# A hybrid decoder layer: SSM output products by pairs of groups, turns of the identity in routing, and a tail that starts two blocks sooner

## The reference

```
h    = rms_norm(x, ln1_g);  proj = h @ w_in
a    = differential attention (4 heads, two softmax maps each, head norm)
c    = GLU, causal depthwise conv (31 taps), LayerNorm, silu
s    = S5 SSM: 16 channel groups x 64 complex states, GELU, GLU
x    = x + concat(a, c, s) @ w_out
h2   = rms_norm(x, ln2_g)
x    = x + MoE(h2)     # top 1 of 4 groups, then top 2 of its 8 experts
out  = rms_norm(x, final_g)
# expert: act = silu(xb @ w_gate[e]) * (xb @ w_up[e]);  y = act @ w_down[e]
```

## Time and profile before

| | |
|---|---|
| runs | 1229.65, 1231.2, 1232.02 us; median 1231.2 |
| the profiled execution | 1231.33 us, span 1229.6 us |
| mean granted clock of TensorE | 0.966 of 2.4 GHz |
| TensorE busy | 1142.1 us, 93% of the span |
| VectorE, ScalarE, GpSimd busy | 466.2, 366.2, 287.9 us |
| SSM output products | 265.6 to 282.6 us |
| routing, last logits to first expert block | 557 to 583.9 us |
| expert blocks | 583.9 to 1199 us |
| tail | 1199 to 1229.6 us |

### The profile page before, as it was taken

One profiled execution on the slowest core, in us unless ns is written; L12 is line 12 of the kernel. 1 busy time (PEld: TensorE's weight loads), 2 busy tenths in 40 slices (PEclk: granted clock), 3 DMA queues, 4 the chain that ended last, 5 costly groups with the idle time before them and its releaser, 6 DMA issues.

```text
span 1229.6 us, 16168 instructions
## 1 busy us (share of the span) xinstructions
PE 1142.1 (93%) x5022; PEld 547.6 (45%) x5023; DVE 466.2 (38%) x1011; ACT 366.2 (30%) x736; POOL 287.9 (23%) x227
## 2 busy tenths in 40 slices
PE   6999999998899999994899999987999999999990
PEld 5897444454346666654233333322333333333330
DVE  3550039942446666446222323312232332322313
ACT  3221100025455556412223232222322223323223
POOL 0110299920000000101022122222212212122123
PEclk9999999999899999997799999989999999999995
DMA  8127111012411111177692999999799999999217
GB/s 254 26 39 140 35 35 35 0 69 74 171 35 59 63 50 37 52 296 298 231 375 31 359 374 375 410 414 413 284 364 378 396 404 378 404 361 409 99 21 276
DMA packets 86157, 261.95 MB, mean 213 GB/s; under 512 B 31927, under 2 KB 49086, under 8 KB 61518
## 3 DMA queue, kind: packets, MB, share of 16 engines
q1 hardware_dynamic: 68868, 243.43, 51.6%
q0 software_dynamic: 11520, 16.81, 6.2%
q10 hardware_dynamic: 5706, 0.92, 0.4%
HBM read 244.86 MB, written 26.74 MB: 221 GB/s over the span
## 4 chain that ended last, share of the span: by engine, by line
PE 88%; DMA 5%; ACT 2%; DVE 2%; issue 1%; POOL 0%; SPq 0%; DVEq 0%; ACTq 0%; POOLq 0%
PE psum L1349 28%; PE psum L1368 14%; PE psum L1058 13%; PE psum L1248 9%; PE psum L1055 4%; PE psum L1202 3%; DMA W<-in_w_gate 3%; PE psum L1335 3%; PE psum L1222 3%; PE psum L1053 2%; PE psum L1356 2%; PE psum L1213 2%; PE psum L1277 1%; DMA W<-in_x 1%; PE psum L1266 1%
## 5 line engine op out<-in xcount | busy, mean ns | idle before, releaser
L1349 PE MATMUL psum<-W,RD 128*64 (+1 forms) x800 | 371.9, 609 | 15.4 <-DVE RD L1869 14.5
L1350 PE MATMUL psum<-W,RD 128*64 128x512 f32 x800 | 371.9, 609 | 0.0
L1349 PEld LDWEIGHTS psum<-W,RD 128*64 128x64 f32 x800 | 107.4, 140 | 229.0 <-issue 223.1
L1368 PE MATMUL psum<-W,RD 128*64 (+1 forms) x400 | 184.0, 603 | 2.3 <-ACT RD L981 2.3
L709 POOL DMA_INDIRECT x_rows<-RD,tabi x49 | 79.7, 1627 | 452.2 <-ACT RD L988 442.5
L1369 PE MATMUL psum<-RD 128*64 128x512 f32 x400 | 184.0, 603 | 0.0
L1851 DVE TENSOR_TENSOR RD<-psum,RD 128x256 f32<-128x256 f32 x50 | 21.3, 425 | 420.6 <-ACT RD L977 420.6
L1058 PE MATMUL psum<-W 128*128 128x512 f32 x384 | 166.4, 593 | 0.6 <-ACT W L794 0.6
L1248 PE MATMUL psum<-W,RD 128*128 128x512 f32 x256 | 119.9, 602 | 1.6 <-ACT RD L870 1.1
L1058 PEld LDWEIGHTS psum<-W 128*128 128x128 f32 x384 | 72.5, 190 | 89.7 <-issue 88.7
L1350 PEld LDWEIGHTS psum<-W,RD 128*64 128x64 f32 x800 | 107.4, 140 | 0.0
(11 more groups left out here) (324 smaller groups left out, 1269.3 us busy)
## 6 DMA issues: line engine op xcount, KB each, us to landing
W<-in_w_up SPq DMA_DIRECT2D x32, 2048.0 KB, 13.3
W<-in_w_gate SPq DMA_DIRECT2D x32, 2048.0 KB, 18.2
W<-in_w_down SPq DMA_DIRECT2D x32, 2048.0 KB, 20.1
W<-in_x SPq DMA_DIRECT2D x16, 512.0 KB, 4.7
W<-in_w_in SPq DMA_DIRECT2D x5, 1024.0 KB, 11.6
W<-in_w_in SPq DMA_DIRECT2D x16, 256.0 KB, 4.3
x_rows<-W SPq DMA_DIRECT2D x8, 512.0 KB, 2.9
h_rows<-RD SPq DMA_DIRECT2D x8, 512.0 KB, 3.6
```

What stands on the lines that cost most here:

```text
L1349: pe.matmul(bank(2)[0:HALF].rearrange("p (g n) -> p g n", g=2), x, near, start=k == 0, stop=k == KD - 1)
L1350: ins = pe.matmul(bank(2)[HALF:P], x, upgate1[:, k].rearrange("p g n -> p (g n)"), start=k == 0, stop=k == KD - 1)
L1368: pe.matmul(out[0:HALF], a, W[:, bass.ds(base + (2 * KD * FF + D * k), 512)], start=k == 0, stop=k == FK - 1)
```

## The change

Three parts.

1. The SSM output products go by pairs: for pair `a` first both groups' `XR` products, then both `XI` products, then both `TG` products. The sums and their places in PSUM are the same.
2. `spin(count)` issues so many turns of the identity into a PSUM bank that nobody reads: 36 behind the rank counts, 24 behind the four column turns. Two semaphores (`col_ok`, `col_ps`) are folded into `tab_ok` and `tab_ps`.
3. `block_io(b)` scatters block b-2 instead of b-1, ahead of the gather, so that the last two blocks are never scattered. SyncE loads the tiles of the tail when the scatters up to the third last block have landed (`sent` and `got` hold their counts). VectorE squares tiles 0 to 3 and ScalarE tiles 4 to 7. All eight tiles are scaled and stored, also rows that are not final. Apart from that GpSimd fetches the 128 half rows of the second last block (`rows_in(0)`), VectorE adds that block's output, GpSimd writes them back to `x2_rows`, fetches the rows of the last block (`rows_in(1)`), VectorE adds the last block's output straight from PSUM with its gate. Both row tiles are squared, the two halves of each token's mean are added across partitions, rooted and scaled with a half-wise copy of the gain (`fgh`), and written over the stored rows of `out` once all bulk stores have landed: `rows_out(0)`, then `rows_out(1)`.

```diff
+            out_half = t["out"][0].rearrange("n (h d) -> (n h) d", h=2)
             def block_io(b):
+                if b >= 2:
+                    pool.wait_ge(ex_ye, b - 1)
+                    if b >= 3:
+                        pool.wait_ge(scat_out[(b - 1) % 2], 16 * ((b - 1) // 2))
+                    add_rows(tabi[:, b - 2:b - 1], yb[b % 2], scat_out[b % 2])
                 pool.wait_ge(ex_xT, b + 1)
                 gather(b + AHEAD)
-                if b:
-                    pool.wait_ge(ex_ye, b)
-                    if b >= 2:
-                        pool.wait_ge(scat_out[b % 2], 16 * (b // 2))
-                    add_rows(tabi[:, b - 1:b], yb[(b - 1) % 2], scat_out[(b - 1) % 2])
...
-            sp.wait_ge(moe_done, 3 + AHEAD)
+            sp.wait_ge(scat_out[0], sent[0])
+            sp.wait_ge(scat_out[1], sent[1])
             for i in range(NT):
-                sp.dma_start(x3[:, i, :], x2_dram[i * P:(i + 1) * P, :]).then_inc(x3_in[i], 16)
+                sp.dma_start(x3[:, i, :], x2_dram[i * P:(i + 1) * P, :]).then_inc(x_in[i], 16)
...
+            pool.wait_ge(cur_c, 2)
+            for s in range(2):
+                pool.wait_ge(scat_out[s], got[AHEAD + s])
+            rows_in(0)
+            for i in range(4):
+                tile_root(i)
+            pool.wait_ge(yrow_ok[0], 1)
+            for i in range(NT):
+                pool.wait_ge(x_in[i], 32)
+            pool.indirect_dma_start(x2_half, bass.IndirectOffsetOnAxis(ap=cur[:, 0:1], axis=0), yrow[0], None,
+                                    bounds_check=2 * L - 1, oob_is_err=False).then_inc(scat_m, 16)
+            tile_root(4)
+            tile_root(5)
+            tile_root(6)
+            tile_root(7)
+            pool.wait_ge(scat_m, 16)
+            rows_in(1)
+            row_root(0)
+            pool.wait_ge(orow_ok, 1)
+            pool.wait_ge(fin_out, 16 * NT)
+            rows_out(0)
+            row_root(1)
+            pool.wait_ge(orow_ok, 2)
+            pool.wait_ge(row_out[0], 16)
+            rows_out(1)
...
-            y_evac(ylast, bank(6), act.snap(more + (EXPERTS - 1)), act.snap(more + EXPERTS), 0, None, tail_y)
-            for i in range(NT):
...
+            for i in range(4, NT):
+                act.wait_ge(x_in[i], 32)
...
+                act.activation(banks(2, 2), x3[:, i, :], ACT.Square, accum_out=ms3[:, i:i + 1]).then_inc(ms3_ok, 1)
...
+            for r in range(2):
+                act.wait_ge(yrow_ok[r], 1)
...
+                act.activation(bank(3), yrow[r], ACT.Square, accum_out=msx[:, r:r + 1]).then_inc(sqx_ok, 1)
...
-            for g in range(GROUPS):
...
+            for a in range(PAIRS):
+                out = [psum[:, 2 * r + a // 4, P * (a % 4):P * (a % 4) + P] for r in range(2)]
+                for X, CA, first in ((XR, CAR, True), (XI, CAI, False)):
+                    for r in range(2):
+                        q = slice(STATES * r, STATES * r + STATES)
+                        pe.matmul(out[r], X[q, a, :], CA[q, a, 1:CHUNK + 1, :].rearrange("p t h -> p (t h)"),
+                                  start=first, stop=False)
+                for r in range(2):
+                    ins = pe.matmul(out[r], UT[:, 2 * a + r, :], TG[:, 2 * a + r, :], start=False, stop=True)
+                if a % 4 == 3:
                     ins.then_inc(y_ps, 1)
...
+            def spin(count):
+                for _ in range(count):
+                    pe.transpose(bank(6)[:, 0:P], ident[:, :], ident[:, :])
...
             ins.then_inc(rank_ps, 1)
+            pe.wait_ge(head_ss, NI)
+            spin(36)
...
-            ins.then_inc(col_ps, 1)
+            ins.then_inc(tab_ps, 1)
+            spin(24)
...
+            for i in range(4):
+                dve.wait_ge(x_in[i], 32)
+                dve.tensor_tensor_reduce(out=sqjunk, in0=x3[:, i, :], in1=x3[:, i, :], scale=1.0, scalar=0.0,
+                                         op0=ALU.mult, op1=ALU.add, accum_out=ms3[:, i:i + 1]).then_inc(ms3d_ok, 1)
+                dve.wait_ge(ms3d_ok, i + 1)
+                tile_mean(i)
+            dve.wait_ge(xrow_in[0], 16)
+            dve.wait_ge(ex_ye, dve.snap(more + (EXPERTS - 1)))
+            dve.tensor_tensor(yrow[0], RD[:, bass.ds(odd_at + 3072, 512)], xrow[0], ALU.add).then_inc(yrow_ok[0], 1)
+            for i in range(NT):
+                if i >= 2 and i + 2 < NT:
+                    dve.wait_ge(ms3_ok, i - 1)
+                    tile_mean(i + 2)
+                tile_scale(i)
+            row_mean(0)
+            dve.wait_ge(xrow_in[1], 16)
+            dve.wait_ge(ex_y, dve.snap(more + EXPERTS))
+            dve.wait_ge(glast_ok, 1)
+            dve.scalar_tensor_tensor(yrow[1], bank(6), glast[:, :], xrow[1], ALU.mult, ALU.add).then_inc(yrow_ok[1], 1)
+            row_scale(0)
+            row_mean(1)
+            row_scale(1)
```

More of the change, by code:

```diff
@@ L223, in build @@
         x3 = W[:, 2 * SLOT:2 * SLOT + NT * D].rearrange("p (t n) -> p t n", t=NT)
+        late = W[:, 2 * SLOT + NT * D:3 * SLOT]
+        xrow = [late[:, 0:512], late[:, 512:1024]]
+        yrow = [late[:, 1024:1536], late[:, 1536:2048]]
+        orow = [late[:, 2048:2560], late[:, 2560:3072]]
+        sqjunk = late[:, 3072:4096]
+        fgh = xr[:, 512:1024]
         def slot_up(s):
@@ L292, in build @@
         rstd3 = sb("rstd3", [P, NT])
+        msx = sb("msx", [P, 2])
+        mvx = sb("mvx", [P, 4])
+        rsx = sb("rsx", [P, 2])
+        glast = sb("glast", [P, 1])
         hss = sb("hss", [P, HEADS, NT])
@@ L440, in build @@
         x2_out = [sem(f"x2_out{i}") for i in range(3)]
-        tail_y = sem("tail_y")
         scat_out = [sem(f"scat_out{i}") for i in range(2)]
-        scat_last = sem("scat_last")
-        moe_done = sem("moe_done")
+        xrow_in = [sem(f"xrow_in{i}") for i in range(2)]
+        yrow_ok = [sem(f"yrow_ok{i}") for i in range(2)]
+        scat_m = sem("scat_m")
+        glast_ok = sem("glast_ok")
+        sqx_ok = sem("sqx_ok")
+        mvx_ok = sem("mvx_ok")
+        rsx_ok = sem("rsx_ok")
+        orow_ok = sem("orow_ok")
+        row_out = [sem(f"row_out{i}") for i in range(2)]
+        ms3d_ok = sem("ms3d_ok")
         fg_in = sem("fg_in")
-        x3_in = [sem(f"x3_in{i}") for i in range(NT)]
         ms3_ok = sem("ms3_ok")
@@ L596, in last_of @@
                 return sp.value_load(ends[0:1, p:p + 1], min_val=1, max_val=MAXBLK)
+            sent = [sp.value_load(counts_i[0:1, 1 + AHEAD + s:2 + AHEAD + s], min_val=16, max_val=16 * MAXBLK) for s in range(2)]
             gone = {}
@@ L738, in _ @@
             extra(0)
[L739 removed]
+            for r in range(2):
+                pool.tensor_copy(cur[:, r:r + 1], tabi[:, bass.ds(more + (EXPERTS - 2 + r), 1)]).then_inc(cur_c, 1)
             got = [pool.value_load(counts_i[0:1, 1 + n:2 + n], min_val=16, max_val=16 * MAXBLK) for n in range(AHEAD + 2)]
[L741 to L743 removed]
@@ L744, in _, with rows_in @@
[L744 to L750, removed]
-            for i in range(NT):
+            def rows_in(r):
+                pool.indirect_dma_start(xrow[r], None, x2_half, bass.IndirectOffsetOnAxis(ap=cur[:, r:r + 1], axis=0),
+                                        bounds_check=2 * L - 1, oob_is_err=False).then_inc(xrow_in[r], 16)
@@ new lines, in _ @@
+            tile_root(4)
[12 more added lines that the diff above has]
+            rows_out(1)
+            for n, done in enumerate(gather_in):
+                pool.wait_ge(done, got[n])
@@ L756, in _ @@
+            pool.wait_ge(row_out[1], 16)
         @block.scalar
@@ L1019, in _ @@
             extra(0)
-            y_evac(ylast, bank(6), act.snap(more + (EXPERTS - 1)), act.snap(more + EXPERTS), 0, None, tail_y)
[L1022 to L1026, removed]
+            act.activation(glast[:, :], tabg[:, bass.ds(more + (EXPERTS - 1), 1)], ACT.Copy).then_inc(glast_ok, 1)
+            for i in range(4, NT):
+                act.wait_ge(x_in[i], 32)
+                if i > 4:
+                    act.wait_ge(ms3_ok, i - 4)
+                act.activation(banks(2, 2), x3[:, i, :], ACT.Square, accum_out=ms3[:, i:i + 1]).then_inc(ms3_ok, 1)
+            act.wait_ge(ms3_ok, 4)
+            for r in range(2):
+                act.wait_ge(yrow_ok[r], 1)
+                if r:
+                    act.wait_ge(sqx_ok, 1)
+                act.activation(bank(3), yrow[r], ACT.Square, accum_out=msx[:, r:r + 1]).then_inc(sqx_ok, 1)
         @block.tensor
@@ L1817, in _ @@
             link(dve.scalar_tensor_tensor(third, third, -float(SLOTS), pos, ALU.mult, ALU.add))
-            dve.tensor_scalar(col[:, 0:1], third, float(SLOT), None, ALU.mult).then_inc(col_ok, 1)
+            dve.tensor_scalar(col[:, 0:1], third, float(SLOT), None, ALU.mult).then_inc(tab_ok, 1)
             dve.wait_ge(tab_ps, 1)
@@ L1892, in _ @@
             dve.wait_ge(fg_in, 16)
[L1893 to L1899, removed]
+            dve.tensor_copy(fgh[0:HALF], fgb[0:HALF, 0:512])
@@ new lines, in _, with tile_mean, tile_scale @@
```

(7 more changed lines are left out.)

34 lines of the change are left out of this document (24 added, 10 removed).

## The result

The changed kernel takes 1216.97 us in the median of four runs (1214.88 to 1218.94), against 1230.76 before: ratio 0.9888, 95% interval 0.9873 to 0.9902, 13.8 us less. The forecast was 1212.8, range 1207 to 1220. The profiled execution took 1218.94 with a span of 1217.2, one of the slower of its runs; it is 12.4 us of span shorter than before.

The account below looks back on a forecast made before the run. TensorE was taken to bound the kernel, with 88% of the chain that ended last. 1231.33 - 6.6 (SSM products) - 3.6 (turns) - 8.2 (tail) = 1212.9; median 0.1 below, 1212.8 us; range 1207 to 1220.

Parts of the forecast that it names:

- SSM products: SSM output products on TensorE: by pairs, 1.27 instead of 2.10 us per pair, 6.6 us less over 8 pairs.
- Rival 2: SSM output products: the halves run one after the other, 3.4 us lost, 1216.2 us; chance 0.10.
- the scores: Attention score products, the same 64-row form, where two of 128 columns take 0.42 us together; basis for overlapping halves.
- The margin for GELU: Behind the SSM products: GELU ends 2.3 us before TensorE's next unit, and this margin stays.
- Turns: Routing: identity turns raise TensorE's clock, 2.0 us less in the tables and 1.6 in block 0, 3.6 together.
- Rival 1: Routing: the turns don't raise the clock, 3.6 + 0.7 us lost, 1217.1 us; chance 0.17.
- Tail: Behind the expert loop: loads issued sooner and last two blocks not scattered, end at 1221.4 instead of 1229.6, 8.2 us less.
- end 0.8 later as before: Tail: the kernel ends 0.8 us after the last row transfer lands at 1220.6, so at 1221.4.
- the bulk stores landing 5.2 us after the last issue: Tail: the last bulk store lands at 1211.6, 5.2 us after issue, and the row transfers to `out` follow.
- rival 3: Tail: row transfers share the DMA with the bulk and become the chain, gain 1.9, 1219.1 us in all; chance 0.13.
- "TensorE's last block is not touched by" the loads: End of the expert loop: the tail's tile loads don't affect TensorE's last block, which reads no more weights from HBM.
- The 10 us to spare: Tail: the last down product has some 10 us to spare, so neither its clock nor its eviction counts.

Follow-up runs that it names:

- e1_old_products: The changed kernel with the SSM output products group by group again, as in the kernel before; 1223.24 us, ratio 0.9945.
- e4_more_turns: The changed kernel with 58 turns instead of 36, 40 instead of 24, and 8 more behind the first turn of rows; 1215.88 us, ratio 0.9884.
- a_again: The changed kernel itself, unaltered, measured and profiled a second time; 1215.97 us, ratio 0.9886.
- e5_drain_sooner: The changed kernel with GpSimd's gather waits ahead of its last row transfer and no wait for that transfer to land; 1214.52 us, ratio 0.987.
- e7_turns_and_drain: The changed kernel with the turns of e4_more_turns and the sooner drain of e5_drain_sooner together; 1213.75 us, ratio 0.987.
- e6_loads_late: The changed kernel with SyncE's eight tail loads also waiting for the last block's turned activation to be evicted; 1223.79 us, ratio 0.9944.

## Why the prediction was right or wrong

The time was 1216.97 (1215.97 the second time) against 1212.8, inside the range; the gain was 13.8 us where 18.0 was forecast. By its own steps:

**SSM products.** Forecast 6.6 us, 1.27 a pair; the profile has 1.29 a pair and 6.7, the medians of e1_old_products 6.3 to 7.3. Rival 2 (the halves one after the other, 3.2) is out: the scores were the right rows. The margin for GELU held too: GELU ends at 280.5 and the unit behind the products at 282.8, 2.3 us later, as before.

**Turns.** Forecast 3.6 us as 2.0 for the tables and 1.6 for block 0. The medians give 3.3 to 4.3, the profiles a mean of 3.2 at the scatter of block 47. The parts: tables held at the high clock take 4.5 to 4.8 us from their start instead of 6.4 to 6.5, 1.7 to 2.0 less, and 5.7 where the clock falls in between. Block 0 gains 0 to 2.8. That the sum came out near 3.6 is in part luck: it is a mean over executions that gain from about 0 to 6, and what happens to block 1 and the loop behind it was in no step. Rival 1 is out: with the clock at 0.50 and nothing but turns behind the rank counts, it rose. The Trainium skill's rule (TensorE: Matmul & The Clock Gate, Part 4: PE-mode transpose) that a transpose doesn't count as TensorE being busy disagrees with the trace here for rising as well as for holding: e4_more_turns has 1.00 from 560 to the end of block 0, through its turns, where the kernel before fell to 0.50 at 582.9 behind an idle time of 4.44. What I didn't see is that the profile of one execution can't price this part: 34.6 to block 1 in one profile of the changed kernel, 31.1 in the other.

**Tail.** Forecast 8.2 us, measured 3.2 in the profile, 2.6 to 3.6 in the medians and 3.0 to 4.5 over all profiles. This is the term that was mis-sized. Nearly all of the miss is one term: "end 0.8 later as before". Shifted by the 9.17 us that TensorE was ahead (1180.45 to 1171.28), the forecast had the last row transfer landed at 1220.6 - 9.17 = 1211.4; it landed by 1211.0. From there to the end it was 6.2 and not 0.8, 5.4 more, against 5.0 missed in all (the transfers themselves were 0.4 early): the drain. The kernel before had a drain of 6.4 us that hid behind the last bulk stores. I took the distance from the last store to the end as fixed, when it was SyncE's distance and not GpSimd's. GpSimd became the last engine by this change, so its own closing had to be looked up.

Inside the chain two steps were wrong and cancelled. I had the bulk stores landing 5.2 us after the last issue, at 1202.4 on the shifted scale, and the rows to `out` waiting for them. They land after 2.7 to 4.1 now; why they are quicker, no run isolates. Instead the rows of block 49 came late, at 1202.47 where I had 1200.1, mostly because the last tile load landed 15.5 us after the first issue and not 13 to 14; their fetch took 5.1 among the stores. So a part of rival 3 is what happened (the fetch of these rows is in the chain), at 5.1 instead of 8.8. The write-back is not: it took 5.2 here and 2.8 in a_again, and the fetch follows it by 6.0 us in both, behind GpSimd's roots. The two transfers to `out` took 2.8 and 2.4, with no traffic beside them, where I had 3.7: a plain write isn't priced by the accumulating scatter. "TensorE's last block is not touched by" the loads was wrong as well: it was held up by 4.44. The 10 us to spare that I had counted there took it in, and it cost nothing.

**What no step had.** The clock in attention gave this execution about 1.1 us. Summed for the profiled execution: 6.7 + 1.1 + 1.2 in routing (35.74 - 34.57 until block 1) + 0.2 in the loop (582.37 - 582.12 until the scatter of block 47) + 3.2 = 12.4, the difference of the spans. The 1.2 in routing isn't all due to the turns: 0.4 of it is that the rows of h2 landed sooner (3.94 instead of 4.41), so that VectorE began sooner and the tables started 7.88 instead of 8.33 behind the rank counts.

## What to carry to other kernels

When a change lets another engine finish last, price that engine's closing as well: here GpSimd's drain of 5.8 us, which stood in the profile of before, hidden. Let a transfer be waited for by an engine that closes cheaply, and let GpSimd start its drain at issue. If waits are filled with turns, fill them up to the next real product: with pauses of 1.7 and 0.9 us left in this kernel, block 0 had the low clock throughout, in part or not at all. Follow what is gained to a point far behind it, since the next wait can take it back, and look at more than one profile before pricing it.

## What the runs showed of the hardware that was not expected

- GpSimd's closing drain takes 5.79 us when it starts behind a landed transfer (5789 ns in eight profiles), and ends 5.8 us after GpSimd's last instruction also with that transfer in flight (e5_drain_sooner, e7_turns_and_drain), against 0.01 for SyncE and 0.75 to 0.8 for ScalarE and VectorE in the same kernels.
- TensorE's clock rose from 1.2 to 2.4 GHz within 36 turns of the identity (at about 557 in the changed kernel, from 0.50 to 1.00), and was at 1.00 from there through the rest of 58 turns, the tables and 40 turns (e4_more_turns).
- Eight tile loads of 0.5 MB held TensorE's next instructions up by 2.4 to 4.4 us, without any data that it needed from them.
- An indirect plain write of 128 rows of 2 KB to `out` landed in 2.4 to 2.8 us in quiet. The write-back beside the bulk stores took 2.8 us in seven profiles and 4.9 to 5.3 in three, so the bulk stores alone don't explain the longer time. The fetch of as many rows took 3.5 with the loads moved away (e6_loads_late), 5.1 to 5.3 beside the stores and 7.7 to 9.0 beside the tile loads. The accumulating write took 3.3 at least.
